# Expert blocks of a mixture-of-experts step: gathered rows turned ahead of the up products, rows split ahead of the weights, gated products last

## The reference, cut to what matters

```python
def expert_block(args):
    tok, e = args
    xb = x2d[tok]
    hb = jax.nn.silu(xb @ exp_w1[e]) * (xb @ exp_w3[e])
    return hb @ exp_w2[e]

routed = segment_sum(yb.reshape(P, D) * slot_w[:, None], slot_tok, num_segments=N)
```

## Time and profile before

| | |
|---|---|
| median of 3 runs | 2332.51 us (2324.74 to 2335.27) |
| profiled execution | 2333.93 us, its span 2332.2 us |
| PE, DVE, ACT, POOL busy | 86%, 54%, 43%, 29% of the span |
| DMA, mean over the span | 181 GB/s |
| expert stage, first to last end of down products | 1041.3 to 2257.1 us of the span |

### The profile page before, as it was taken

The page is one execution under the profiler, slowest core; times in us unless marked ns, Lnnn a source line. Parts: engine busy times, 40 slices in busy tenths (PEclk is TensorE's granted clock), DMA queues, the critical chain, the costliest instruction groups (busy, mean ns, idle before and its releaser), DMA issues. The chain is left out here.

```text
span 2332.2 us, 31175 instructions
## 1 busy us (share of the span) xinstructions
PE 1996.4 (86%) x8459; PEld 1323.3 (57%) x8460; DVE 1268.9 (54%) x2023; ACT 1012.2 (43%) x1458; POOL 678.6 (29%) x643
## 2 busy tenths in 40 slices
PE   6697888999789799249999999999999998999970
PEld 1344444468687444137676676676666665666740
DVE  2566345101777588635565555566555455556646
ACT  2244533101223111036665565666655555565641
POOL 4111000000000125513434444343444444444440
PEclk9699999999999899579999999999999999999985
DMA  9343100110000542079789989767888989987465
GB/s 298 108 157 118 55 18 18 45 37 19 10 1 1 210 165 91 19 298 320 213 244 307 329 257 304 212 174 229 238 275 262 352 261 316 314 274 218 108 179 190
DMA packets 110114, 422.47 MB, mean 181 GB/s; under 512 B 19300, under 2 KB 33636, under 8 KB 85100
## 3 DMA queue, kind: packets, MB, share of 16 engines
q1 hardware_dynamic: 62508, 261.05, 30.1%
q0 software_dynamic: 47248, 160.70, 27.0%
q10 hardware_dynamic: 304, 0.02, 0.0%
HBM read 336.61 MB, written 85.66 MB: 181 GB/s over the span
## 5 line engine op out<-in xcount | busy, mean ns | idle before, releaser
L1765 DVE TENSOR_TENSOR wupl<-w,wuph 128x2048 fp32r<-128x2048 f32 x232 | 521.4, 2289 | 546.0 <-ACT wuph L1731 532.3
L1731 ACT ACTIVATE wuph<-w 128x2048 fp32r x232 | 432.0, 1916 | 40.3 <-SPq L1555 37.4
L1682 PE MATMUL bank<-w,hT 128*128 x912 | 412.7, 595 | 1.0 <-issue 0.9
L1664 PE MATMUL bank<-wuph,xTh 128*128 128x512 f32 x920 | 370.1, 402 | 20.4 <-DVE xTl L1774 20.3
L1664 PE MATMUL bank<-wuph,xTl 128*128 128x512 f32 x920 | 362.2, 394 | 0.0
L1664 PE MATMUL bank<-wupl,xTh 128*128 128x512 f32 x920 | 360.9, 392 | 0.0
L1682 PEld LDWEIGHTS bank<-w,hT 128*128 128x128 f32 x912 | 164.4, 190 | 168.9 <-issue 168.6
L1616 POOL DMA_INDIRECT xg<-hn_scratch,idx_g x118 | 212.3, 1799 | 95.5 <-POOL idx_g L1608 92.6
L1721 ACT ACTIVATE y<-bank 128x512 f32<-128x512 f32 x114 | 68.1, 598 | 355.2 <-POOLq L1621 190.8
L1624 POOL DMA_INDIRECT yacc_scratch<-y,idx_s x114 | 185.8, 1630 | 113.9 <-ACT y L1722 62.0
L1664 PEld LDWEIGHTS bank<-wuph,xTh 128*128 128x128 f32 x920 | 174.7, 190 | 58.7 <-issue 25.1
(11 more groups left out here) (315 smaller groups left out, 2254.5 us busy)
## 6 DMA issues: line engine op xcount, KB each, us to landing
w<-in_exp_w SPq DMA_DIRECT2D x192, 1024.0 KB
wada<-in_w_ada POOLq DMA_DIRECT2D x16, 1024.0 KB, 6.9
wg<-in_w_in SPq DMA_DIRECT2D x12, 1024.0 KB, 5.9
wada<-in_w_ada SPq DMA_DIRECT2D x4, 2048.0 KB, 14.8
yacc_scratch<-zero POOLq DMA_DIRECT2D x10, 512.0 KB, 8.4
x<-x_scratch SPq DMA_DIRECT2D x9, 512.0 KB
x_scratch<-x SPq DMA_DIRECT2D x9, 512.0 KB, 2.6
hn_scratch<-hn SPq DMA_DIRECT2D x9, 512.0 KB
```

What stands on the lines that cost most here:

```text
L1664: mm = pe.matmul(b_up[j][:, :], x[:, k, :], w[:, :, k, :], start=(k == 0 and i == 0), stop=(k == KT - 1 and i == 2))
L1682: mm = pe.matmul(b_down[half][:, :], hT[:, i, :], w2[:, bass.ds(slot, 1), i, half * 512:(half + 1) * 512].rearrange("p s n -> p (s n)"), s ...
L1731: act.activation(part13(wup[j][0], half), raw13(e % WSLOT, half), ACT.Copy).then_inc(w_high, 1)
L1765: dve.tensor_tensor(part13(wup[j][1], half), raw13(e % WSLOT, half), part13(wup[j][0], half).bitcast(F32), ALU.subtract).then_inc(w_low, 1)
```

## The change

It changes the order of the calls in the loop over pairs of blocks on three queues. No instruction, wait, count or buffer changes; the prologue, POOL and SP stay as they are.

- PE: `turn(b+2)` goes in front of `up(b+1)`, right behind `turn_h(b)`; it stood between `up(b+1)` and `down(b)`.
- ACT: `xt(b+2)` goes in front of `high(b+2)` and `silu(b+1)`; it stood behind both.
- DVE: `x_low(b+2)` goes in front of `low(b+2)`; so `hidden(b+1)` is the last.

```diff
             with pe.Fori(0, n) as r:
                 for u in range(2):
                     turn_h(r * 2 + u, u)
+                    turn(r * 2 + (u + 2), u)
                     up(r * 2 + (u + 1), 1 - u)
-                    turn(r * 2 + (u + 2), u)
                     down(r * 2 + u, u)
...
             with act.Fori(0, n) as r:
                 for u in range(2):
                     ht(r * 2 + u)
+                    xt(r * 2 + (u + 2), u)
                     high(r * 2 + (u + 2), u)
                     silu(r * 2 + (u + 1), 1 - u)
-                    xt(r * 2 + (u + 2), u)
                     y_half(r * 2 + u, u)
...
             with dve.Fori(0, n) as r:
                 for u in range(2):
+                    x_low(r * 2 + (u + 2), u)
                     low(r * 2 + (u + 2), u)
                     hidden(r * 2 + (u + 1), 1 - u)
-                    x_low(r * 2 + (u + 2), u)
```

## The result

The changed kernel takes **2,410.3 us** (median) against 2,333.9 us before: a ratio of 1.0326, 95% interval 1.0294 to 1.0358, so 76 us slower. One of its four executions was disturbed (3,089.55 us): it is counted in this median, which would be 2,405.8 us without it, and not in the ratio. The profiled execution has a span of 2,400.7 us.

A forecast was written before the change was run, and what follows sets the result against it. In the expert stage's crowded stretches POOL's chain (scatter, landing, gather, scatter) was taken to set the pace, elsewhere PE's work. 54 - 20.3 + 14 = +48 us on 2,332.5 gave 2,380 us; range 2,334 to 2,418 us.

The forecast's parts named there:

- The gather is wanted 5.6 us earlier: PE's row transposes: every block wants its gather 5.6 us earlier; gather waits go from 26 us to over 80 us.
- The lock's term: POOL's gather issue: held up by one 2.25 us piece of VectorE's weight subtraction per late gather, 24 times, +54 us.
- The low rows: VectorE's low half of the rows ahead of the weights: PE's 24 waits for it go, -20.3 us.
- The gated products last: End of VectorE's queue: high rows first delay weights and gated products, using up the cover in calm blocks, +14 us.
- The clock: PE in the expert stage: longer waits may bring a few more falls to half clock; none counted in the sum.
- rival 1: POOL keeps its times; gather waits only replace other stalls: +3 us, 2,336 us, no change; chance 0.12.
- rival 2: PE's gathers arrive early enough, only the low rows' waits go: faster, 2,312 us; chance 0.05.
- rival 3: Gated products bound every block, 0.3 us in each of 113, 34 us, also outside the crowd: 2,366 us; chance 0.09.

The follow-up runs named there:

- e5: The changed kernel with POOL issuing gathers one scatter earlier (gather b+5, then scatter b, instead of gather b+4): 2,342.1 us, ratio 1.0031.
- e6: The kernel before with only PE's queue order changed and POOL issuing gathers one scatter earlier: 2,335.8 us, ratio 1.0035.
- e3: The kernel before with each piece of the weight subtraction in the loop cut from 2,048 to 256 columns: 2,289.5 us, ratio 0.9806.
- e4: The changed kernel with each piece of the weight subtraction in the loop cut from 2,048 to 256 columns: 2,314.5 us, ratio 0.9895.
- e7: The kernel before with each piece of the weight subtraction made in four instructions of 512 columns: 2,313.5 us, ratio 0.9932.
- e8: The changed kernel with each piece of the weight subtraction made in four instructions of 512 columns: 2,338.3 us, ratio 1.0021.
- e1: The kernel before with only PE's queue changed (row turn ahead of the up products), ScalarE and VectorE in the old order: 2,371.1 us, ratio 1.0158.
- e11: The kernel before with each piece of the weight subtraction made in eight instructions of 256 columns: 2,349.3 us, ratio 1.0068.

## Why the prediction was right in its direction and short in its size

The forecast was 2,380 us and slower; the measured time, 2,410 us, lies in the range, 30 us over the forecast, where the rivals lie below it. Step by step:

- **The gather is wanted 5.6 us earlier.** Right. e5 and e6, which only let the gathers leave earlier, take nearly all of the loss away, by PE's waits and by POOL's scatter steps together. PE's wait of 98.4 us in 36 blocks, up to 4.8 us, is what was foreseen (over 80 us, over 35 blocks, up to 5 us).
- **The lock's term, +54 us.** Its size came out near by luck, and its place is wrong. The prediction had a late gather drag one piece of the subtraction over the issue of the next gather, 24 times 2.25 us, with a median of over 2 us for that issue. The median fell to 1.00 us, and the gather's two steps got 136 us shorter; the scatter's two steps pay (236.7 to 303.0 us). What a subtraction that POOL can get past leaves of the 76 us is 21 to 25 us, in two pairs of kernels (e3 and e4, e7 and e8), so some 50 us need the long subtraction. Why the subtraction meets the scatter's steps more often isn't settled: e1 has it without the drag. Nor is it settled why e1, with nearly as much time in these steps, loses only 37 us; its trace has 858.0 us from the ends of the scatters' issues to the next copies, where the kernel before has 879.9 us, and with that its smaller loss fits.
- **The low rows, -20.3 us.** Right: the wait is gone.
- **The gated products last, +14 us.** Too much for the changed kernel. The weight load waits in 87 blocks instead of 24, but for 31.2 us instead of 22.4, PE's own wait is 4.4 us shorter, and the calm blocks take 10.0 us. The cover is used up as worked out; while PE waits for gathers, little is seen of it. In e5, without those waits, PE idles 61.9 us for the gated products.
- **The clock, none in the sum.** This term was left at zero without a reason. Waits of 3 us and more were foreseen, and with them that the clock falls; it stood at half in 24 stretches, and PE's busy time grew by 25.1 us. The Trainium skill ("TensorE: Matmul & The Clock Gate", HAM oscillation) names this way of losing time, and this trace agrees: 0.79 of the clock in the window with the 3.54 us wait.
- **Which term the 30 us belong to stays open.** The clock's 25.1 us of busy time are near the 30 us that the forecast lacks, but no kernel here has the waits without the slow clock. e5 has 11 such stretches, 44.4 us together, and is only 7 to 10 us slower than the kernel before, so the slow clock isn't paid in full there. And seen from POOL, the scatter's steps and the waits ahead of its issue grew by 74.1 us, which is the whole loss, where the lock's term had 54.
- **The rivals.** POOL's times aren't kept (rival 1): its chain got longer by the scatter's steps. Nothing speaks for rival 2, since 36 gathers came late, and for rival 3 the calm blocks would have had to be longer.

## What to carry to other kernels

Moving a consumer forward in its queue moves the deadline of everything it waits for: before doing it, compare the new deadline with the landing times in the crowded stretches, not with the calm ones, and move the producer forward in its queue too. Where PE waits in a loop, look for the slow clock behind each long wait as well, and don't leave it at zero; how much of it reaches the total depends on what else sets the pace. Where long VectorE instructions with both inputs in SBUF stand beside POOL's small copies and indirect DMA issues, try them in shorter pieces, as long as VectorE has the time to spare: here four pieces of 0.69 us gave 0.7%, eight of 0.42 us lost 0.7%.

## What the runs showed of the hardware that was not expected

An indirect DMA's issue on POOL is held up while VectorE subtracts two SBUF operands. With the queues in the order of before, the gather's issue took 1.81 us in the mean beside pieces of 2.29 us, 1.10 beside pieces of 0.69, and 1.00 us in e3, where they cover 256 columns. All 69 issues of over 1.3 us in the kernel before overlap a piece, and e3 and e11 have no issue that long. POOL gets in between pieces that follow each other without a gap: in e7, 39 of the 111 shorter gather issues lie for more than half of their time beside a piece. The Trainium skill ("SBUF — State Buffer", Who interferes with whom) infers that such a subtraction leaves descriptor generation alone; for the indirect gather these runs show otherwise. Whether it is the descriptors or the reading of the token list from SBUF that is held up, no run here tells.
